# Second attention of a three-layer network: the first rope on GpSimd, two score steps ahead of the last query unit, later preparation

## What is computed

```python
q, kc, vc, ks, vs, kw, vw, gl = split_cols(u @ w_in, C_WIDTHS)
q = partial_rope(q.reshape(b, s, C_HEADS, HEAD_DIM), cos, sin)   # first 16 of 64 columns are rotated
kc, ks, kw = (partial_rope(kv(k), cos, sin) for k in (kc, ks, kw))
# compressed branch: 32 tokens at a stride of 16 become one key and one value
kc = gelu(windows(kc + pe_k) @ wk1) @ wk2        # 15 keys; vc likewise
o_c = masked_softmax(q @ kc * scale) @ vc
o_s = masked_softmax(q @ ks * scale) @ vs        # selected blocks: with 256 tokens, all of them
o_w = masked_softmax(q @ kw * scale) @ vw        # window of 512: with 256 tokens, all of it
out = gate0 * o_c + gate1 * o_s + gate2 * o_w
```

## Time and profile before

| | us |
|---|---|
| three runs | 899.15, 899.81, 900.08 |
| median | 899.81 |
| the profiled execution's own time | 899.29 |
| its span | 897.5 |
| TensorE busy in the span | 883.0 (98%) |
| VectorE busy | 643.4 (72%) |
| ScalarE busy | 509.8 (57%) |
| GpSimd busy | 132.2 (15%) |

### The profile page before, as it was taken

How to read it: one execution, slowest core, us unless ns; L and a number is a source line. 1 busy time by engine, 2 the same in 40 slices (tenths; PEclk the granted TensorE clock), 3 DMA queues, 4 the chain that set the end, 5 groups by cost and what they waited for, 6 DMA issues and landing times. The chain is left out here.

```text
span 897.5 us, 14768 instructions
## 1 busy us (share of the span) xinstructions
PE 883.0 (98%) x4748; PEld 734.5 (82%) x4748; DVE 643.4 (72%) x1313; ACT 509.8 (57%) x1021; POOL 132.2 (15%) x176
## 2 busy tenths in 40 slices
PE   8999999999999999999999999999999999999998
PEld 7878678888888888888888888888887778878876
DVE  4768857666666689786476666666976878787785
ACT  6655746444444475685454444444666666566573
POOL 1310600000000000454010000000620401400401
PEclk9999999999999999999999999999999999999999
DMA  9643144655566547011447665655464445454531
GB/s 341 228 151 114 49 164 144 230 188 190 191 193 195 193 165 236 23 48 49 140 133 224 191 198 191 188 189 188 148 204 142 154 144 172 155 173 142 168 115 48
DMA packets 41610, 145.75 MB, mean 162 GB/s; under 512 B 4689, under 2 KB 6225, under 8 KB 41553
## 3 DMA queue, kind: packets, MB, share of 16 engines
q1 hardware_dynamic: 41264, 144.93, 49.0%
q10 hardware_dynamic: 288, 0.07, 0.0%
HBM read 143.93 MB, written 1.05 MB: 162 GB/s over the span
## 5 line engine op out<-in xcount | busy, mean ns | idle before, releaser
L474 DVE TENSOR_TENSOR wl<-raw,wh 128x1024 fp32r<-128x1024 f32 (+2 forms) x270 | 328.7, 1222 | 86.7 <-ACT wh L469 84.2
L469 ACT ACTIVATE wh<-raw 128x1024 fp32r<-128x1024 f32 (+2 forms) x270 | 281.4, 1046 | 61.9 <-PE acc L357 47.0
L355 PE MATMUL acc<-wh,xhl 128*128 128x512 f32 (+1 forms) x472 | 190.9, 404 | 1.3 <-DVE wl L474 0.9
L357 PE MATMUL acc<-wh,xhl 128*128 128x512 f32 (+1 forms) x472 | 184.4, 391 | 0.0
L356 PE MATMUL acc<-wl,xhl 128*128 128x512 f32 (+1 forms) x472 | 183.9, 390 | 0.0
L355 PEld LDWEIGHTS acc<-wh,xhl 128*128 128x128 f32 x472 | 88.7, 188 | 26.0 <-issue 8.3
L357 PEld LDWEIGHTS acc<-wh,xhl 128*128 128x128 f32 x472 | 88.6, 188 | 19.2
L356 PEld LDWEIGHTS acc<-wl,xhl 128*128 128x128 f32 x472 | 88.8, 188 | 16.3
L355 PE MATMUL acc<-wh,hh 128*128 128x512 f32 x256 | 100.2, 392 | 0.0
L356 PE MATMUL acc<-wl,hh 128*128 128x512 f32 x256 | 100.0, 391 | 0.0
L357 PE MATMUL acc<-wh,hl 128*128 128x512 f32 x256 | 99.6, 389 | 0.0
(11 more groups left out here) (333 smaller groups left out, 1357.6 us busy)
## 6 DMA issues: line engine op xcount, KB each, us to landing
raw<-stream SPq DMA_DIRECT2D x266, 512.0 KB, 3.5
raw<-stream SPq DMA_DIRECT2D x4, 352.0 KB, 5.8
h<-x SPq DMA_DIRECT2D x4, 256.0 KB, 3.9
out<-h SPq DMA_DIRECT2D x3, 256.0 KB, 2.1
row<-rows SPq DMA_DIRECT2D x1, 700.0 KB, 9.2
probs<-sel SPq DMA_DIRECT2D x1, 512.0 KB, 8.1
cst<-consts SPq DMA_DIRECT2D x1, 507.0 KB, 7.3
out<-h SPq DMA_DIRECT2D x2, 128.0 KB, 2.1
```

What stands on the lines that cost most here:

```text
L355: nc.tensor.matmul(out_, ah, bh, start=start, stop=False, skip_group_check=True)
L357: return nc.tensor.matmul(out_, al, bh, start=False, stop=stop_, skip_group_check=True)
L469: nc.scalar.activation(used(u, wh[:, u % SPLIT, :]), used(u, raw[:, u % RAW, :]), ACT.Copy).then_inc(w_hi, 1)
L474: nc.vector.tensor_tensor(used(u, wl[:, u % SPLIT, :]), used(u, raw[:, u % RAW, :]), used(u, wh[:, u % SPLIT, :]).bitcast(F32), ALU.subtra ...
```

## The change

Four things are moved; nothing is added to the computation or taken from it.

1. The rope of the first eight heads is done by GpSimd, ahead of its loop over the steps, and no longer by VectorE.
2. TensorE's two turns of these heads come one after the last compression unit, the other after the first key unit; before, they came after the third and the fourth compression unit. `q_high` on ScalarE follows: the first after all four splits of that stretch, the second after the tanh of the compressed keys.
3. The scores of step 1 come ahead of the last query unit, together with those of step 0. ScalarE takes step 1's exponentials in its iteration 2, and the evacuation of the last query group comes one iteration later.
4. The first compressed scores come at the end of step 3 and not in its middle; the turns of the last eight heads move from steps 3 and 5 to 4 and 6, their halves from 4 and 6 to 5 and 7, the compressed scores of the last heads from 7 and 8 to 8 and 9, and the softmax over the compressed keys one step later. The three early splits come at ScalarE's iterations 6, 8, 10 (before 7, 9, 13) and VectorE's 8, 9, 12 (before 8, 11, 14).

```diff
-        CO_HIGH, CO_LOW = (7, 9, 13), (8, 11, 14)
+        CO_HIGH, CO_LOW = (6, 8, 10), (8, 9, 12)
...  TensorE
                 last.then_inc(w_used, 1)
-                if k >= 2:
-                    query_blocks(k - 2)
+            query_blocks(0)
 
             def compressed(uu):
 
                 n = CG * N_CMP
+                if uu == 0:
+                    query_blocks(1)
...
-                if it == 3:
-                    pe.wait_ge(dve_prep, 10)
-                    pe.wait_ge(ev_act, left(G_CO))
-                    pe.wait_ge(ev_dve, left(G_CO))
-                    compressed_scores(range(0, 4))
                 if it < STEPS_C:
                     c_scores(it)
-                if it == 8:
+                if it == 9:
                     compressed_scores(range(12, 16))
...
+                if it == 3:
+                    pe.wait_ge(dve_prep, 10)
+                    pe.wait_ge(ev_act, left(G_CO))
+                    pe.wait_ge(ev_dve, left(G_CO))
+                    compressed_scores(range(0, 4))
                 if it == 4:
                     compressed_scores(range(4, 8))
-                if it == 7:
+                if it == 8:
                     pe.wait_ge(q_lo, 12)
                     compressed_scores(range(8, 12))
-                if it in (3, 5):
-                    z = (it + 1) // 2
+                if it in (4, 6):
+                    z = it // 2
...
-                if it == 14:
+                if it == 15:
                     pe.wait_ge(dve_prep, 11)
...
                     c_iter(0)
-                if uu == 3:
                     c_iter(1)
...  ScalarE
             for uu in range(4):
                 split(U_CMP + uu + LEAD)
-                if uu == 2:
-                    q_high(0, Z_C)
-            q_high(1, Z_C + 1)
+            q_high(0, Z_C)
             split(U_CK + LEAD)
             act.wait_ge(dve_mid, 2)
             s_.activation(gy, gy, ACT.Tanh, scale=0.7978845608028654).then_inc(act_prep, 1)
+            q_high(1, Z_C + 1)
...
-                if it == 3:
-                    exponentials(STEPS_AB + 1)
-                if it != 2 and it - 1 < STEPS_C:
+                if it - 1 < STEPS_C:
                     exponentials(STEPS_AB + it - 1)
...
-                if it == 1:
+                if it == 2:
                     evac(act, G_C + 3, U_CQ2 + 4, 0, Y[:, 0, CQ + GW:CQ + 2 * GW], rr(N_A1), GW)
-                if it in (4, 6):
+                if it in (5, 7):
                     q_high(it // 2, Z_C + it // 2 + 1)
...  GpSimd
-            pool.wait_ge(dve_prep, 6)
+            pool.wait_ge(dve_prep, 7)
+            pool.wait_ge(ev_act, left(G_C + 2))
+            pool.wait_ge(ev_dve, left(G_C + 2))
+            rope(g, pc_, heads_of(Y[:, :, CQ:CQ + GW], 8), 8, vaf[:, 512:1024], q_roped)
...  VectorE
-            dve.wait_ge(dve_prep, 7)
-            dve.wait_ge(ev_act, left(G_C + 2))
-            dve.wait_ge(ev_dve, left(G_C + 2))
-            rope(v_, ch, heads_of(Y[:, :, CQ:CQ + GW], 8), 8, tmp, q_roped)
             for uu in range(4):
                 split(U_CMP + uu + LEAD)
...
+                if it == STEPS_C:
+                    dve.wait_ge(pe_prep, 5)
+                    v_.tensor_copy(pct[:, :], acc[3][:, :]).then_inc(dve_prep, 1)
...
-                if it in (4, 6):
-                    q_low(it // 2, Z_C + it // 2 + 1, 4 + it)
+                if it in (5, 7):
+                    q_low(it // 2, Z_C + it // 2 + 1, 3 + it)
```

More of the change, by code:

```diff
@@ L1757, in _ @@
                     act_turn_block(act, 3, ccs=(it - STEPS_C,))
-                if it == 1:
+                if it == 2:
                     evac(act, G_C + 3, U_CQ2 + 4, 0, Y[:, 0, CQ + GW:CQ + 2 * GW], rr(N_A1), GW)
-                if it in (4, 6):
+                if it in (5, 7):
                     q_high(it // 2, Z_C + it // 2 + 1)
-                if it == 11:
+                if it == 12:
                     act.wait_ge(dve_mid, 3)
@@ L2486, in _ @@
                     dve_turn_block(dve, 3, ccs=(it - STEPS_C,))
-                if it in (4, 6):
-                    q_low(it // 2, Z_C + it // 2 + 1, 4 + it)
-                if it in (5, 9):
-                    b = it // 9
+                if it in (5, 7):
+                    q_low(it // 2, Z_C + it // 2 + 1, 3 + it)
+                if it in (6, 10):
+                    b = it // 10
                     dve.wait_ge(cmp_scored, b + 1)
@@ L2494, in _ @@
                         v_.tensor_reduce(pc5[:, t, b], parts[:, t], AX.X, ALU.add).then_inc(parts_added, 1)
-                if it == 10:
+                if it == 11:
                     dve.wait_ge(parts_added, 2 * T)
@@ L2499, in _ @@
                     v_.tensor_tensor(pcall, pcall, over_keys, ALU.subtract).then_inc(dve_mid, 1)
-                if it == 12:
+                if it == 13:
                     dve.wait_ge(act_prep, 5)
@@ L2503, in _ @@
                     ch.link(v_.tensor_scalar(cmx, cmx, 1e-30, None, ALU.max))
-                if it == 13:
+                if it == 14:
                     ch.link(v_.reciprocal(cmx, cmx))
@@ L2507, in _ @@
                     v_.tensor_tensor(pcall, pcall, over_keys, ALU.mult).then_inc(dve_prep, 1)
-                if it == 15:
-                    dve.wait_ge(pe_prep, 5)
-                    v_.tensor_copy(pct[:, :], acc[3][:, :]).then_inc(dve_prep, 1)
             dve.wait_ge(dve_prep, 12)
```

## The result

The changed kernel takes **904.22 us** (median of 9 runs, 903.07 to 909.45), the kernel before beside it 899.44 (9 runs, 899.04 to 901.45): ratio 1.0068, 95% interval 1.0053 to 1.0083. It is slower by 4.8 us, where +2.1 was forecast. Five of its nine runs took 903.07 to 904.22 and four 907.65 to 909.45, so the median is the longest of the lower five; the experiment "The change again" bears on what parts them. The time is within the range; it is near that of the rival "the clock falls" (904.1, given 0.18) and not that of the forecast (901.9, given 0.56). The profiled execution took 904.22 us, span 902.3, at a mean granted clock of 0.996.

The account below looks back on a forecast made before the run. TensorE, busy 883.0 of 897.5 us, was taken as the limit. The sum was 899.29 + 3.17 (rope stall) - 1.1 (steps) = 901.4, with the median's 0.52 901.9 us; range 898.6 to 904.4, the forecast's own 900.7 to 903.1.

Parts of the forecast that it names:

- the clock falls: Rival: TensorE's 4.2 us stall brings back the slower clock, costing 2.2 more, 904.1 us; chance 0.18.
- What bounds: Whole kernel: TensorE is the limit, busy 883.0 of 897.5 us, so only its waits matter.
- the compression units: Second attention: the fourth unit's weights are ready at 339.0, so TensorE runs it without a wait, to 340.63.
- The rope on GpSimd: Beside VectorE's splits: instructions alternate, the first turn waits 4.2 us until 344.86, everything behind is 3.17 late.
- not held up: Rival: GpSimd reads between a split's elements, queries are ready at 340.63, 897.6 us; chance 0.12.
- keeps its turn: Rival: GpSimd's four queued multiplies run consecutively after the first split, lateness 0.8, 899.5 us; chance 0.14.
- The steps: Sixteen head steps: waits removed gain 0.50, 0.59, 0.5 and 0.5, two later blocks cost 0.5 each; 1.1 gained.
- The two waits of 0.5 for ScalarE's copy: Near steps 6 and 8: query-block evacuations stand before ScalarE's copy, costing TensorE about 0.5 each.
- the opening's ten matmuls: Kernel start, out of rest: ten matmuls at 0.46 each against 0.24, used to price the clock rival at 2.2.

Follow-up runs that it names:

- The change again: The changed kernel unaltered, run again: 904.62 us (6 runs), single profiled runs 908.12, 907.96, 908.68 and 904.16, and 903.66 us (6 runs).
- the steps alone: Kernel before with only parts 3 and 4 of the change: 898.62 us (before 899.51), ratio 0.9992.
- the rope alone: Kernel before with the rope moved to GpSimd and the two turns moved as in the change: 904.57 us (before 899.55), ratio 1.0048.
- the wait on VectorE: Rope on VectorE after its first split, both turns after the fourth compression unit, plus a TensorE wait for VectorE's fourth gelu operation: 904.41 us, ratio 1.0049.
- the clock held up: The changed kernel with 16 matmuls of zeros on TensorE ahead of the first turn: 901.54 us (before 899.55), ratio 1.0014; again 901.70.
- behind the first split: The changed kernel with the rope on VectorE after its first compression split, both turns after the fourth compression unit: 897.63 us (before 899.51), ratio 0.9987.
- the rope ahead of the splits: The changed kernel with the rope back on VectorE before its four compression splits: 898.92 us (before 899.55), ratio 0.9984.
- the splits held: The changed kernel with VectorE waiting for GpSimd's rope before its second compression split: 899.32 us (before 899.55), ratio 0.999.

## Why the prediction was wrong

*What bounds, and the compression units: right.* The fourth unit runs without a wait, as forecast.

*The rope on GpSimd: right, and nearly to the tenth.* Forecast were multiplies of about 5.5, the rope's end at 344.8 and the turn at 344.86 after a wait of 4.2; measured 5.47, 344.36 + 0.50 = 344.86, and 344.91 after 4.01. The steps between blocked instructions, 0.31 and 1.09 by the two places of the trace, came as 0.32 and 1.08, and they carried it. The rule of the Trainium skill, "SBUF — State Buffer", section "Who interferes with whom", that a VectorE instruction with two SBUF inputs and a GpSimd instruction that reads SBUF exclude each other, agrees with the trace: 5.47 beside four splits, 2.54 beside one. What the rule alone doesn't give is who comes next, and that the rows did. The rivals "not held up" and "keeps its turn" fall.

*The steps: right in kind, 0.83 for 1.1* (1.03 with the steps alone). The two waits of 0.5 for ScalarE's copy came (385.05, 391.67), and those at the first steps went.

*The clock: the step that failed.* The prediction put it as a rival with 0.18, and in its sum took the stall's price as idle time alone, "everything behind is late by" 3.17; the clock stood there at nothing. In fact the clock fell to 0.50 in each of the nine traces with a stall of 4.0 to 4.5 us: seven of the change, one of the rope alone, one of the wait on VectorE. In the other runs of these kernels the mean clock, never above 0.998, agrees. In the profiled execution the fall cost 2.37 beside the stall's 3.22. The rival's size was right: 2.2 by the opening's ten matmuls, 1.5 to 2.5 measured for the first fall. Its chance was the error, not its price.

That the median, 904.22, lies 0.1 from the rival's 904.1 is partly luck: four of the nine runs had times and mean clocks like those with a second fall, which lifted it, and the 15 runs of the change below 905 have their median at 903.57. The prediction's own text spoke for the rival: it noted that no wait of TensorE before was as long and that only the opening, out of rest, had the half pace. So "1.00 everywhere" was no evidence on a wait of 4 us, and the one place behind a resting TensorE had the slow pace. (That place is evidence by its pace alone: the clock column reads 1.00 there, from 0 to 8 us of the trace of before.) The sentence of the Trainium skill, "TensorE: Matmul & The Clock Gate", Part 1, that the default is throttled and activity releases it, agrees with the trace (0.50 behind 4.01 us without a matmul) and should have weighed more.

With the clock held up the forecast's sum came out: +1.99 measured, +2.07 forecast. That it fits to a tenth is luck too, since the interval of that run is 0.0 to 2.5 us; by its trace the two terms are 3.10 (taken from the first compression unit on) and 0.83.

*The spread.* Nothing in the prediction had the second fall in the steps, which takes some runs of the change to 908, and by their times and mean clocks others to 909. What sets it off is open; 4 of the 91 runs of before also lie some 4 to 5 us above their median, with a mean clock of 0.994.

## What to carry to other kernels

Price a long stall of TensorE twice, as idle time and as the slower clock behind it: here 4.0 us of waiting cost 3.2 net of what it replaced and 1.5 to 2.5 more afterwards. Work moved to GpSimd was not free here, with VectorE running two-input instructions from SBUF beside it, even though GpSimd was idle; put the small operation between VectorE's own blocks, at the place where the next consumer is still covered (behind the first split: 897.63), before giving it away.

## What the runs showed of the hardware that was not expected

The granted clock fell to 0.50 not only at a wait of 4 us but also, in three traced runs, in a stretch where TensorE's longest waits were two of 0.52, and stayed there for some 10 us with TensorE busy throughout. Waits of 1.26 (the rope ahead of the splits) and of 0.78 and 0.60 (the splits held) left it at 1.00 in the profiled runs.
